# Multiplying raw activations by the norm's weight and applying each token's RMS factor when banks are emptied

## What is computed

```
def rms_norm(x, g):
    xf = x.astype(jnp.float32)
    y = xf * lax.rsqrt(jnp.mean(xf * xf, axis=-1, keepdims=True) + EPS)
    return (y * g.astype(jnp.float32)).astype(x.dtype)

def conv_ffn(h, w_in, conv_w, conv_b, w_out):      # layers 2 and 3
    s = h.shape[1]
    u = h @ w_in
    up = jnp.pad(u, ((0, 0), (CONV_WIDTH - 1, 0), (0, 0)))
    c = conv_b + conv_w[0] * up[:, 0:s]
    for i in range(1, CONV_WIDTH):
        c = c + conv_w[i] * up[:, i:i + s]
    a, gate_in = jnp.split(c, 2, axis=-1)
    return (jax.nn.silu(a) * gate_in) @ w_out
...
    h = h + conv_ffn(rms_norm(h, norm_ffn[layer]), ...)
```

## Time and profile before

| | us |
|---|---|
| median of 3 runs | 1906.36 |
| lowest and highest | 1884.24, 1908.88 |
| the profiled execution, its own time | 1904.0 |
| its span, first to last instruction | 1902.2 |
| mean granted PE clock in it | 0.946 |

### The profile page before, as it was taken

The page is one execution under the profiler, slowest core; times in us unless marked ns, Lnnn a source line. Parts: engine busy times, 40 slices in busy tenths (PEclk is TensorE's granted clock), DMA queues, the critical chain, the costliest instruction groups (busy, mean ns, idle before and its releaser), DMA issues. The chain is left out here.

```text
span 1902.2 us, 31934 instructions
## 1 busy us (share of the span) xinstructions
PE 1822.7 (96%) x13818; PEld 1726.2 (91%) x13818; DVE 1194.6 (63%) x1860; ACT 911.6 (48%) x1279; POOL 0.2 (0%) x4
## 2 busy tenths in 40 slices
PE   6999999999999899999999999899999999999998
PEld 6889999999999899999999988677899998789998
DVE  5798546566557987366666454535477647557763
ACT  5544454555445634545554333224555534455552
POOL 0000000000000000000000000000000000000000
PEclk9999999999999999999999999658999998599999
DMA  6520035455544300354555425000245543035551
GB/s 234 178 89 1 23 130 195 141 177 181 197 138 174 111 23 1 111 188 146 177 180 196 170 110 203 23 1 1 89 178 183 196 176 117 1 105 183 191 186 67
DMA packets 34843, 245.92 MB, mean 129 GB/s; under 512 B 3856, under 2 KB 4240, under 8 KB 5392
## 3 DMA queue, kind: packets, MB, share of 16 engines
q1 hardware_dynamic: 34704, 243.89, 36.1%
HBM read 242.83 MB, written 1.05 MB: 128 GB/s over the span
## 5 line engine op out<-in xcount | busy, mean ns | idle before, releaser
L337 PE MATMUL PS<-XH,WH 128*128 128x256 f32 (+1 forms) x2664 | 768.2, 288 | 27.7 <-DVE XL L1535 23.4
L337 PE MATMUL PS<-XL,WH 128*128 128x256 f32 (+1 forms) x2664 | 759.5, 285 | 0.0
L337 PE MATMUL PS<-XH,WL 128*128 128x256 f32 (+1 forms) x2664 | 759.0, 285 | 0.0
L1535 DVE TENSOR_TENSOR WL<-RAW,WH 128x2048 fp32r<-128x2048 f32 x226 | 509.8, 2264 | 338.4 <-ACT WH L1009 338.3
L337 PEld LDWEIGHTS PS<-XH,WH 128*128 128x128 f32 (+1 forms) x2664 | 515.1, 193 | 34.1 <-DVE XL L1535 21.9
L1009 ACT CAST WH<-RAW 128x2048 fp32r<-128x2048 f32 x226 | 425.2, 1883 | 202.7 <-PE PS L337 179.2
L337 PEld LDWEIGHTS PS<-XL,WH 128*128 128x128 f32 (+1 forms) x2664 | 515.4, 193 | 2.3 <-issue 1.6
L337 PEld LDWEIGHTS PS<-XH,WL 128*128 128x128 f32 (+1 forms) x2664 | 515.1, 193 | 0.3
L337 PE MATMUL PS<-INH,WL 128*128 128x256 f32 x832 | 233.8, 281 | 0.0
L337 PE MATMUL PS<-INH,WH 128*128 128x256 f32 x832 | 233.0, 280 | 0.0
L337 PE MATMUL PS<-INL,WH 128*128 128x256 f32 x832 | 231.3, 278 | 0.0
(11 more groups left out here) (122 smaller groups left out, 1559.0 us busy)
## 6 DMA issues: line engine op xcount, KB each, us to landing
RAW<-w_in SPq DMA_DIRECT2D x52, 1024.0 KB, 4.9
RAW<-w_up SPq DMA_DIRECT2D x44, 1024.0 KB, 4.8
RAW<-f_in SPq DMA_DIRECT2D x44, 1024.0 KB, 4.9
RAW<-w_down SPq DMA_DIRECT2D x22, 1024.0 KB, 4.8
RAW<-f_out SPq DMA_DIRECT2D x22, 1024.0 KB, 5.2
RAW<-a_w_in SPq DMA_DIRECT2D x10, 1024.0 KB, 5.0
RAW<-w_out SPq DMA_DIRECT2D x8, 1024.0 KB, 4.8
RAW<-w_bdn SPq DMA_DIRECT2D x4, 1024.0 KB, 5.7
```

What stands on the lines that cost most here:

```text
L337: return e.matmul(out, l, r, start=start, stop=stop, skip_group_check=True)
L1535: e.tensor_tensor(out, x, y, op).then_inc(*V.up(*key, of=of))
```

## The change

Every stage now multiplies the unnormed X times the norm's weight: ACT writes XH = X * weight (`upper`), DVE writes XL = X * weight - XH (`lower`), both as soon as a part of X is complete, so that no input of a stage waits for the factor `rs`. The factor is applied by DVE when a bank is emptied (`scaled`): the bank times rs, into SBUF. Since the taps must see scaled values, all taps now read this SBUF copy. ACT does two taps of each part (one of them into a second buffer with `e.mul`), DVE adds the second buffer, and does the remaining tap(s). The squares are added over the four parts on DVE (`squares`), and PE needs two matmuls of ones for each norm (`square_sum`, in front of the products k = 6 of the stage's first chunk) where it needed eight. A short transpose (`rs_turned`) gives the factor per partition where a product is token-major. For attention the factor goes into the tables of the rotary angles. The norm between the two blocks is folded (`WFN`, `n1`, `n2`). The outputs of mixers go to INH/INL, those of attention to new buffers XH2/XL2, so that they don't collide with the early XH and XL. At the start the parameters are loaded ahead of X.

```diff
+            def upper(st, n, added, free):
+                waits(added, *free)
+                for k in (2 * n, 2 * n + 1):
+                    s = slice(k * 256, k * 256 + 256)
+                    e.mul(halves_of(st)[0][:, s], X[:, s], norm_gain(st, k)).then_inc(*A.up("x hi", st, k))
...
+            def lower(st, n):
+                xh, xl = halves_of(st)
+                for k in (2 * n, 2 * n + 1):
+                    s = slice(k * 256, k * 256 + 256)
+                    w.wait_ge(*A["x hi", st, k])
+                    stt(xl[:, s], X[:, s], norm_gain(st, k), xh[:, s].bitcast(F), ALU.mult, ALU.subtract, "x lo", st, k)
+
+            def squares(st, n, tiles=SQ, name=None, key="sq"):
+                name = name or st
+                if n == 0:
+                    return
+                w.wait_ge(*A[(key, st, n) if key == "sq" else (key, n)])
+                if n > 1:
+                    w.wait_ge(*V["sq sum", name, n - 1])
+                tt(tiles[0], tiles[0], tiles[n], ALU.add, "sq sum", name, n)
...
+            def scaled(out, bank, *key):
+                w.wait_ge(*P["ps", *bank])
+                tt(v3(out, 2), v3(ps[bank][:, :], 2), rs2, ALU.mult, *key, of=ps.out(*bank))
```

In `down` on DVE, for each of the four parts n:

```diff
                 for n in range(4):
                     added(st, n, (st, "down", n))
+                    if nxt == "s":
+                        lower("sk", n)
+                    elif nxt != "fin2":
+                        lower(nxt, n)
+                    squares(nxt, n)
```

`ffn2` on ACT and on DVE:

```diff
                 for c in range(11):
                     chunk()
-                    chunk()
-                    b = F2[c % 3]
-                    for part, name in enumerate("au"):
-                        w.wait_ge(*P["ps", st, name, c, 0])
+                    if c:
+                        upper_in(c - 1)
+                    b, x, t = F2[c % 3], FR[c % 2], FT[c % 2]
+                    for part in range(2):
+                        waits(V["scaled", st, c, part], *f0)
...
+                            act(b[:, s], x[:, s], ACT.Identity, "tap", st, c, part,
+                                bias=par("ffn_conv_b_2", l * 44 + f), scale=par("ffn_conv_w_2", l * 132 + 88 + f))
+                            e.mul(t[:, s], x[:, s], par("ffn_conv_w_2", l * 132 + 44 + f)).then_inc(*A.up("tap", st, c, part))
+                        if part == 0:
+                            chunk()
                     w.wait_ge(*V["conv", st, c, 0])
                     act(b[:, 1024:1536], b[:, 0:512], ACT.Silu, "gate", st, c)
-                    if c:
-                        gate(c - 1)
```

```diff
                 for c in range(11):
-                    chunk(2)
-                    b = F2[c % 3]
-                    for part, name in enumerate("au"):
-                        w.wait_ge(*A["tap", st, c, part])
-                        conv_bank(...)
-                    if c:
-                        gate(c - 1)
+                    x = FR[c % 2]
+                    chunk()
+                    if c:
+                        taps(c - 1, 1)
+                        product(c - 1)
+                    scaled(x[:, 0:512], (st, "a", c, 0), "scaled", st, c, 0)
+                    chunk()
+                    if c:
+                        lower_in(c - 1)
+                    taps(c, 0)
+                    scaled(x[:, 512:1024], (st, "u", c, 0), "scaled", st, c, 1)
```

More of the change, by code:

```diff
@@ L905, in nsa @@
                         av(i - 4)
-                project("no", "no", "g0")
+                project("no", "no", "g0", XH2, XL2)
             def swa():
                 st = "s"
[L910 to L925, removed]
+                feat((st, "kv"), st="sk", xh=XH2, xl=XL2, opens=st)
+                ps.give(st, "kv", 0)
                 def heads_kv():
@@ L996, in tensor @@
             ffn("g1", "fin2")
-            for n in range(4):
-                squares("fin2", n)
-            ps.give("sq", "fin2")
+            square_sum("fin2")
         def scalar(e):
@@ new lines, in down, with conv @@
+                    if nxt == "n":
+                        squares("n", n, SQ2, "n2", "sq2")
+                chunk()
+                if nxt == "s":
+                    for n in range(4):
+                        lower("s", n)
+                V.note("nw", nxt)
+                V.note("f0", nxt)
+            def conv(out, x, t, o, taps, *key):
+                w.wait_ge(*A["tap", *key])
+                tt(v3(out, 2)[:, :, 1:256], v3(out, 2)[:, :, 1:256], v3(t, 2)[:, :, 0:255], ALU.add, "conv 1", *key)
+                lo, hi = max(0, -o), min(256, 256 - o)
+                w.wait_ge(*V["conv 1", *key])
+                for h in range(2):
+                    b = h * 256
+                    stt(out[:, b + lo:b + hi], x[:, b + lo + o:b + hi + o], taps[h], out[:, b + lo:b + hi],
+                        ALU.mult, ALU.add, "conv", *key)
@@ new lines, in taps @@
+                def taps(c, part):
+                    s = slice(part * 512, part * 512 + 512)
+                    conv(F2[c % 3][:, s], FR[c % 2][:, s], FT[c % 2][:, s], -2,
+                         [par("ffn_conv_w_2", l * 132 + part * 22 + f) for f in (2 * c, 2 * c + 1)], st, c, part)
+                for c in range(11):
+                    x = FR[c % 2]
+                    chunk()
+                    if c:
+                        taps(c - 1, 1)
+                        product(c - 1)
+                    if c > 1:
+                        waits(V["conv", st, c - 2, 1], A["tap", st, c - 2, 1])
+                    scaled(x[:, 0:512], (st, "a", c, 0), "scaled", st, c, 0)
+                    chunk()
```

559 lines of the change are left out of this document (295 added, 264 removed).

## The result

| | us |
|---|---|
| kernel before, median of 4 runs | 1907.62 (1884.24 to 1909.04) |
| changed kernel, median of 4 runs | 2057.57 (2054.13 to 2061.26) |
| ratio, 95% interval | 1.081 (1.073 to 1.089) |
| profiled execution of the changed kernel, its span | 2058.6, 2056.8 |

The change makes the kernel 8.1% slower; 2070 was forecast. In this document a ratio compares only executions within 1.5% of a kernel's quickest, while medians and ranges are over all of them. The page of the changed kernel: busy time by engine, the granted clock in 40 slices, the chain that ended last by engine, and the two groups that PE's waits meet.

The account below looks back on a forecast made before the run. The prediction took PE, busy for 96% of the span, as the bound. It summed 1904.0 + 188 (FFN chains) + 31 (mixers) - 50 (norms) = 2073, said 2070 us, range 2020 to 2120.

Parts of the forecast that it names:

- The chain in the FFN blocks: FFN stages: DVE and ACT steps wait for each other, 18.0 us a g block, 14.1 in f; 188 us lost together.
- PE's waits for WL near 190: Expected sign: PE's waits for WL total near 190 us, in g0 some 3 us twice a block.
- rival 3: Clock stays at 0.50 after PE's waits in g blocks, 110 us more, about 2180; chance 0.08.
- The norms: Fewer matmuls of ones and no waiting for the factor at stage starts: 50 us gained together.
- The folded final norm: Final norm between the two blocks, folded: some 2 us gained.
- 7.1 each: Before each of four FFN stages: PE loses 7.1 us of ones matmuls and waits.
- the 2.6 lost at the starts of m1, n and s: Norms behind a `down`: PE waits 1.7 us and pays 0.9, in place of 6.1.
- the start: Start of the run: 4 us gained, as X needs no factor first.
- the 31: Both mixers: 31 us lost, from k 11 later, forget gates and gates' scaling 3, and m0's masks and bounds 2.
- Attention "unchanged": Attention stages were taken as unchanged by the change.
- (1): Rival: casts early enough, DVE and ACT hide behind PE, only the gain stays; about 1860, 2.4% faster; chance 0.05.
- (2): Rival: only the g stages' chain is real and half of it, mixers hidden; about 1930, 1.3% slower; chance 0.05.

Follow-up runs that it names:

- casts moved: Changed kernel with ACT doing both casts of an FFN block together at the block's start: median 1965.96 us, a block of g 14.33 us.
- work added off the chain: Changed kernel with extra ACT copies of X, two a block in g0 behind the casts, one in g1 before the cast of u: 2072.14 us, one execution.
- second experiment: Changed kernel with the same FFN instructions in another order on ACT and DVE, each step ahead of the wait it stood behind: median 1927.96 us.
- With the clock held up on both sides: Four dead products of ones and X added on PE in sparse attention, to the changed kernel (median 2050.55 us) and the kernel before (1866.34).
- both orders with dead products: Changed kernel with FFN stages reordered, mixers' sums of squares later and gate scaling earlier, plus four dead PE products in sparse attention: median 1844.66 us.
- the dead products alone: Kernel before plus four dead products of ones and X on PE at two waits in sparse attention: median 1866.34 us, 0.981 of itself.

## Why the prediction was right, point by point

**The chain in the FFN blocks: right.** Forecast 18.0 and 14.1 us a block, measured 18.16 and 14.15 (the latter between PE's waits of 1.27 us in f0, at 404.33 and 418.48). All steps of the 18.16 are in the rows above; the taps on ACT take 1.80 (1501.93 to 1503.73) instead of the 1.65 that I took from rows of before, and the cast of the inner activation fills just the moment in which ACT would wait for the scaling. The loss against the same work in a better order is 27.0, 26.7, 71.9 and 72.7 us, forecast 26, 26, 68, 68. The two experiments on ACT's queue show the cause: casts moved, 14.33; work added off the chain, nothing. Two sentences of the Trainium skill that the forecast weighed can now be set beside rows. The Trainium skill (ScalarE: Activation LUTs, "What ACT_TABLE_LOAD costs") gave an estimate of 1.78 us for the four taps, and the trace's 1.80 is nearer to it than to my 1.65. The Trainium skill (TensorE: Matmul & The Clock Gate, "Architectural detail: the array is 16x 32x32") has ACT's and DVE's queues strictly in order; the trace agrees: ACT stands idle for 5.08 us ahead of the taps of u, and the next cast starts only behind them.

**PE's waits for WL near 190: too high.** They are 160.9 less the 15.6 at the start, 145. The forecast had the clock fall after the waits without a price (rival 3), and that is right, but then a slower chunk fills a part of each wait: in g0 the clock is 0.92 on the mean, and a block holds waits of 3.29 and some 1.5 us, or one of 3.29, not two of 3. The price was in the block's 18.16 already. The gaps after which rival 3 has the clock fall are not quite those of its rows either: in the kernel before it fell around most gaps of 2.5 to 4 us, but not at the 2.52 us ahead of m1 (558.56).

**The norms: right in kind, a little low.** No gap before f0, f1, g0, g1; gaps of 2.05, 2.96 and 2.18 before m1, n and s, and 3.35 at the end. With the chain gone (second experiment) f0, f1, g0, g1 are 7.6, 14.4, 6.7 and -0.3 us shorter than before, 28 in all. Cut at the same first products, the forecast's shares are 2.3 - 0.9 = 1.4 behind the start of each of the four, 6.1 at the ends of f0, f1 and g0, 2 for the folded norm in f1 and a loss of 1 in g1: 7.5, 9.5, 7.5 and 0.4, or 25. The folded final norm was the term that was off: f1 gained 14.4 - 7.6 = 6.8 more than f0, for 2. PE had waited there twice, 2.60 us (1093.98) and 2.52 (1100.23). At the ends of m0, m1, n and s the forecast's 7.1 each can't be read alone, nor the 2.6 lost at the starts of m1, n and s.

**Mixers: mis-sized.** With those terms and the start, the forecast for the two stages together was 31 - 4 - 2 x 7.1 + 2.6 = +15 (the parts of the 31 add to 30); they got 30 longer. k came 88.3 us after the end of `down` (677.32 - 589.05), not 82.8, and its wait grew to 2.91 only. The step that failed was to put nearly all of the loss on k. PE meets new waits ahead of it, at the sums of squares (4.84 in each mixer) and at the gates' transposes (4.69 in m0, 3.15 in m1), and one behind it at the merge (3.24). The first two in m0:

```profile
48.27 2.08 PE L362 MATMUL PS<-SB,ONES 128*128 128x512 f32 x2 [4.84 <-ACT SB L1015]
...
77.39 0.39 PE L365 MATMUL PS<-C,SB 16*128 16x16 f32 x2 [4.69 <-DVE SB L1549]
```

After such waits the clock is 0.50 for 3.4 to 6.8 us, 23.9 us in m1 in place of 7.6. That a slower chunk costs time here, because no later wait takes it up, is my reading; no run separates it.

**Attention "unchanged": wrong, and it hid the miss in the mixers.** n and s were forecast 9 us shorter by their norms (2 x (7.1 - 2.6)), and were 45 shorter. Over the kernels with the new order n takes 0.44 us more for each us at 0.50 ((303.4 - 237.2) / (181 - 31)), so 32 of n's 32.7 come from 31 us at 0.50 in place of 103, and next to nothing from the norm. With the clock held up on both sides n is 1.2 us shorter (229.5 against 230.8), where 4.5 were forecast, and the whole kernel 2050.55 against 1866.34: the change costs some 184 us, 9.9%, once this is taken out (the kernel before itself differed by 4 us between these two measurements). s was 12.7 shorter. Reordered and both orders with dead products differ by 11.8 us in s for 34 us at 0.50, so by this estimate 6 of the 12.7 come from 41 us at 0.50 in place of 59; what gave the rest stays open.

**The sum.** Forecast 2073 from 1904.0: FFN +163, mixers +15, attention -9. Measured +170, +30 and -45. The first, which decides, holds; the other two misses nearly cancel, and the 2057.57 is closer to 2070 than the working deserves. The rivals fell. (1) holds in the FFN stages with another order of the same instructions, since the busy sums do allow it, but not for the kernel: outside n and s that order took 1498 us and the kernel before 1500, for the mixers lost 26 of the 28 that the FFN stages gained. (2) and (3) fell outright: no half chain, and no whole stage at 0.50.

**A version faster than both** came out of it: both orders and the dead products, 1844.66 us, 0.969 (0.964 to 0.973) of the kernel before. Of these 64 us, the dead products alone give the kernel before 42; the change in its better order gives 22 more. Between the profiled executions of these two it is 33: 12 lie outside n and s and 21 in s, which stood at 0.50 for 21 us in place of 58. Whether the change or chance kept the clock up in s is not shown, so 12 us is what these profiles show for it.

## What to carry to other kernels

When two in-order engines hand work back and forth, lay one period out step by step over both queues; the sum of that chain, not each engine's busy share, says whether the third engine waits. If it comes out too long, first look for a step that stands behind a wait it doesn't need (here a cast behind taps, a scaling behind a cast's remainder) before cutting work: moving instructions alone gave 198 us. And compare stages that no edit touches before reading a difference of the whole.

## What the runs showed of the hardware

The granted clock in sparse attention fell to 0.50 behind a wait of 2.25 us on PE and stayed there for 24 to 181 us, and for 10.2 us in three profiles in which the two waits (2.25 and 2.84) were mostly filled with dead products of 128x512. In window attention it fell in the middle of small products with no wait of 0.2 us on PE from 1680 us on (at 1703.8 us in the changed kernel). With one wait of 1.27 us in every block of 14.15 it stayed at 1.00 through f0 and f1 of the changed kernel; with waits of 3.29 us in g0 and g1 it fell again and again, for 44 and 63 us in all. In dense FFN chunks it was back after 3.4 or 6.8 us each time. DVE was busy for 40.13 us in four blocks with two extra ACT copies of 128x2048 each, for 40.13 us in four with one, and for 40.12 in four of the changed kernel with none, so the copies' traffic cost DVE nothing.
